# Output projection weights split into other places and earlier, gated products moved, and the first down unit put behind the second up columns

## The chip, the cores and the metric

The kernel runs on one core of one Trainium2 chip. The metric is the device time of one execution in microseconds (us); lower is better. The core has five engines with a queue each: TensorE (PE in the profile), VectorE (DVE), ScalarE (ACT), GpSimd (POOL) and SyncE (SP), which here only starts weight loads. Granted clock means the share of TensorE's full 2.4 GHz that the chip allowed in a stretch.

## What is computed

Two layers over 256 tokens of width 1024 in float32. Each layer is a half-step SwiGLU feed-forward block, an attention block with two kinds of heads (8 stick-breaking, 8 chunked with a relative bias), and a second feed-forward block, with a layer norm after each of the three.

```
x  <- LN1(alpha*x + 1/2 * SwiGLU_1(x))          # width 1024 -> 2816 -> 1024
h  = x @ W_in                                   # q,k,v of both kinds of heads
y  = concat(g_A * headRMS(StickBreak(...)), g_B * headRMS(ChunkAttn(...))) @ W_out
x  <- LN2(alpha*x + y)
x  <- LN3(alpha*x + 1/2 * SwiGLU_2(x))
SwiGLU(x) = (silu(x @ w_gate) * (x @ w_up)) @ w_down
```

## The kernel before

**Split weights.** Every product is made of three matmuls on rounded halves: hi*hi, lo*hi, hi*lo. Weights stream in as *units* of 128 x 2048 float32 (1 MB). SP loads a unit into one of three slots of `raw`; ACT writes its rounded copy into a place of `w_hi` (`split_hi`, L422) and DVE the remainder into the same place of `w_lo` (`split_lo`, L753). There are four places. A raw slot may be loaded again once DVE has made the low part of the unit in it (`lo_ready`); a place may be written again once PE has used the unit there (`unit_used`). PE waits on `lo_ready`. Each engine works its queue in the order in which the code is written: all order around the change is by hand.

**Feed-forward block.** `ffn` takes per step j a gate unit, an up unit and a down unit. Gate and up are products of x (48 matmuls with 256 columns for each unit, `columns`); ACT makes the silu, DVE the gated product (`gated`, signals `hf_done`). The first nine down units are multiplied by Strassen's scheme in seven products of 512 columns, `product(m)`, each accumulated in PSUM bank m; DVE forms sums of weights for it (`weight_sums`: `weight_differences` and `weight_additions`, L768 to L774) and sums of h (`h_sums`), and both are split in hi and lo (`split_pure`, `split_differences`, `split_last_parts`, `high_h`, `low_h`). The last two down units are plain (`pair`). In the second to fourth blocks of the program PE takes the second gate and second up unit before the first down unit. In the program's first block (`count == 0`) PE takes gate 0, up 0, gate 1, products 5, 2, 4, 3 of down 0, then up 1, then products 1, 6, 7.

**Attention block.** Twelve units of W_in, interleaved with the attention of both kinds of heads, then four units of W_out (called W0 to W3 below; `rels` in the code). The softmax of the chunked heads goes in six batches b: PE scores, DVE adds the bias and finds the maximum (`scores`), ACT takes the exponential (`softmax_exp`), DVE normalises, PE transposes (`ca_turn`), and DVE (b 0 to 3) or ACT (b 4, 5) copies back (`turned`). The head outputs are normed (`square`, `head_rstd`, `mix`) and split (`mixed_hi`, `mixed_lo`); each part i of four feeds one W_out unit. PE does W0 for all, W1 for all, then W2 and W3 for token block 0, then W2 and W3 for token block 1.

**Layer norm and the next pair of units.** As soon as a token block's sums are in PSUM (`y_done`), DVE and ACT norm it, PE transposes the result (`turn_x`) and takes the next block's first two units together (`first_pair`, `row_products`). These two must already lie in two places: they are split by `split_hi(..., into=...)` and by `split_second_hi`/`split_second_lo`, the second in two halves. On DVE `split_second_lo` stands ahead of `layer_norm`. Inside the last W_out product of token block 1 stands a transpose of the normed token block 0, so that PE waits there for the norm of token block 0.

SP's loads follow in one queue; `back` says after which unit's low part a slot is free. For the second up unit of the second feed-forward block (raw slot 1) that is the low part of W3.

Of the kernel before, what the change touches and what calls it, by code (L numbers as in the profile page):

```python
# [88 lines left out]
SLOT, FILLED, PER_LAYER = unit_slots()  # L89

# [24 lines left out]
def trunk(nc, x_in, xT_in, stream, ln_gb, mix_g, rel_band, out):  # L115
    ctx = ExitStack()
    with ctx:
# [169 lines left out]
        def phase(l, p):  # L287
            return l * 3 + p
# [128 lines left out]
        def _(act):  # L417
# [26 lines left out]
            def split_second_hi(l, filled, after):  # L444

                act.wait_ge(raw_ready[1], loaded(l, 1, filled))
                act.wait_ge(unit_used, used(l, after))
                for c, done in zip(HALVES, (first_hi, hi_ready)):
                    nc.scalar.activation(w_hi[:, at(0, c)], raw[:, 1, c], ACT.Copy).then_inc(done, 1)

            def split_hi_at(l, rel):
                if rel == ATT0 + WIN_UNITS:
                    act.wait_ge(unit_used, used(l, rel - 2))
                split_hi(l, rel, SLOT[rel], FILLED[rel])

# [35 lines left out]
            def ffn(l, f):  # L491
# [7 lines left out]
                def silu_rows(r, tb, done):  # L499

                    act.wait_ge(*((unit_used, used(l, base + 1)) if tb else (row_done, r + 1)))
                    c = slice(tb * 256, tb * 256 + 256)
                    nc.scalar.activation(sg[:, c], bank[4 + tb][:, 256:512], ACT.Silu).then_inc(done, 1)
# [11 lines left out]
                if r < 0:  # L515
# [3 lines left out]
                    split_hi(l, base + 3, 0, first[0] + 1)  # L519
                    first_unit_hi()  # L520
                    high_h(0)
                    split_differences_hi(l, f, 0)
                else:
# [12 lines left out]
                    split_last_parts_hi(l, f, 0)  # L536
                    split_hi(l, base + 5, 2, first[2] + 1)
# [17 lines left out]
                if r < 0:  # L555
                    step(0)
# [20 lines left out]
                if r < 3 * DEPTH - 2:  # L577
                    split_second_hi(l, first[1] + FP, base + 3 * SF + 3)
# [88 lines left out]
            def attention(l):  # L667
# [47 lines left out]
                split_hi_at(l, ATT0 + 12)  # L715
# [4 lines left out]
                split_hi_at(l, ATT0 + 13)  # L720
# [31 lines left out]
        def _(dve):  # L752
# [49 lines left out]
            def split_half_lo(half, slot=0):  # L802
                c = HALVES[half]
                nc.vector.tensor_tensor(w_lo[:, at(0, c)], raw[:, slot, c], w_hi[:, at(0, c)].bitcast(F32),
                                        ALU.subtract).then_inc((first_lo, lo_ready)[half], 1)

            def split_second_lo(l, p, rel):

                dve.wait_ge(first_hi, phase(l, p) + 1)
                split_half_lo(0, 1)  # L810
                dve.wait_ge(hi_ready, l * UNITS + (rel + 1))
                split_half_lo(1, 1)
# [96 lines left out]
            def ffn(l, f):  # L909
# [25 lines left out]
                def gated_rows(r, tb):  # L935
# [4 lines left out]
                                                   in1=bank[4 + tb][:, 0:256], op0=ALU.mult,  # L940
                                                   op1=ALU.mult).then_inc(row_h_done, 1)

                r = 2 * l + f - 1
                if r < 0:
                    split_lo(l, base + 1, 1)
                    split_lo(l, base + 2, 2)
                    weight_sums(l, f, 0, FILLED[base + 1] + 1)
                    gated(0, 1, bank[7], first=True)
                    h_sums(0)
                    split_pure_lo(l, f, 0)  # L950
                    low_h(0)
                    split_differences_lo(l, f, 0)
                    split_lo(l, base + 3, 0)
# [12 lines left out]
                for j in range(2):  # L966
                    split_last_parts_lo(l, base + 3 * j + 4)
                    if j == 0:
                        split_lo(l, base + 3 * j + 5, 2)
                        weight_sums(l, f, j + 1, FILLED[base + 1] + 2 + j)  # L970
# [3 lines left out]
                    gated(j + 1, 3 * j + 3, bank[7 if r >= 0 and j == 0 else 0])  # L974
# [38 lines left out]
                if not last:  # L1013
                    split_second_lo(l, 2 * f + 1, base + FFN_UNITS + 1)
# [74 lines left out]
            def attention(l):  # L1089
# [22 lines left out]
                normalise(l, 3)  # L1112
                turned(l, 2)
                scores(l, 4)
                normalise(l, 4)
                turned(l, 3)
# [3 lines left out]
                split_lo_at(l, ATT0 + 12)  # L1120
# [3 lines left out]
                split_lo_at(l, ATT0 + 13)  # L1124
                split_lo_at(l, ATT0 + 14)
# [4 lines left out]
                split_lo_into(l, ATT0 + 15, 1, 3)  # L1130
                split_lo_into(l, FFN_BASE[1], 0, 1)
                split_second_lo(l, 2, FFN_BASE[1] + 1)
# [18 lines left out]
        def _(pe):  # L1151
# [64 lines left out]
            def row_products(l, rel, tb, other, count, turn=None):  # L1216

                t = slice(tb * P, (tb + 1) * P)
                w = [tile[:, :].rearrange("p (s c) -> p s c", c=at(other).start - at(0).start)
                     for tile in (w_hi, w_lo)]  # L1220
                s, c0 = divmod(at(0).start, at(other).start - at(0).start)
                o = bank[4 + tb][:, :].rearrange("p (s c) -> p s c", s=2)

                def product(x, part, kc, start=False, stop=False):
                    return plain(o, x[:, kc, t], w[part][:, s:s + 2, c0 + kc * 256:c0 + (kc + 1) * 256], start, stop)
# [19 lines left out]
            def first_pair(l, rel, other, count, units):  # L1245

                turn_x(0, count, 1)
                row_products(l, rel, 0, other, count, lambda half: turn_x(1, count, half))
                last_used(count - 1, units)
                row_products(l, rel, 1, other, count)  # L1250
# [41 lines left out]
            def ffn(l, f, count):  # L1292
# [38 lines left out]
                if count == 0:  # L1331
                    first_columns(l, base, count)
                    columns(l, base + 1, 1, bank[7])
                    step(0, start=True)
                else:
                    first_pair(l, base, 1 if f else 3, count, 2 if f else 1)
# [9 lines left out]
                    columns(l, base + 3, 0, bank[7])  # L1346
                    n = strassen(l, f, 0)
                    pe.wait_ge(hlo_done, it(l, f, 0) + 1)
                    pe.wait_ge(lo_part, 2 * n + 1)
                    product(5, True)  # L1350
                    product(2, True)
                    pe.wait_ge(lo_part, 2 * n + 2)
                    product(4, True)
                    product(3, True, parts_used)
                    pe.wait_ge(lo_ready, split(l, base + 4))
                    product(1, True)
                    product(6, True)
                    pe.wait_ge(hf_done, it(l, f, 1) + 1)
                    product(7, True, unit_used)
# [107 lines left out]
            def attention(l):  # L1467
                first_pair(l, ATT0, 3, phase(l, 1), 1)
# [45 lines left out]
                for i in range(2):  # L1514
                    pe.wait_ge(mlo_done, l * 4 + (i + 1))
                    pe.wait_ge(lo_ready, split(l, rels[i]))
                    for tb in range(2):
                        for half in range(2):
# [3 lines left out]
                            last = down(SLOT[rels[i]], xT_hi, xT_lo, 2 * i, (tb,), start=i == 0, halves=(half,))  # L1522
# [5 lines left out]
                for tb in range(2):  # L1528
                    for i in (2, 3):
# [3 lines left out]
                        for half in range(2):  # L1533
                            turn = (tb, i, half) == (1, 3, 1)
                            last = down(3 if i == 3 else SLOT[rels[i]], xT_hi, xT_lo, 2 * i, (tb,), stop=i == 3,
# [73 lines left out]
```

## Time and profile before

| | us |
|---|---|
| three runs, median | 1018.33 |
| lowest, highest | 1015.13, 1020.71 |
| the profiled execution, time | 1017.5 |
| the profiled execution, span in the trace | 1015.8 |
| PE busy in it | 978.3 |
| DVE busy | 809.2 |
| ACT busy | 566.5 |
| POOL busy | 26.5 |

The span runs from the first to the last instruction of the trace; 1.7 us of the execution's time lie around it. Busy time of an engine is the union of its instructions. A matmul's end in the trace is modelled: back to back, 512-column matmuls start 0.23 us apart and show 0.39 us each, so a row's idle time before a matmul is about 0.16 us less than the delay it stands for. The mean granted clock is 0.989. Layer 0 of the trace is roughly 0 to 498 us: feed-forward 0 to 204, attention to 318, feed-forward to 517; layer 1 follows in the same pattern, its attention ending near 815 us.

### The profile page before, as it was taken

How to read it: one execution, taken by the hardware profiler on the slowest of the kernel's cores; microseconds unless marked ns; L12 is line 12 of the kernel's file. 1: busy time of each engine (PE TensorE's matmuls, PEld its weight loads, DVE VectorE, ACT ScalarE, POOL GpSimd, SP SyncE). 2: the span in 40 equal slices, each digit the busy share in tenths (PEclk: the TensorE clock that was granted, in tenths of full speed). 3: DMA queues.
4: the chain of work that ended last, by engine and by line, in shares of the span. 5: the costliest groups of instructions: out<-in, count | busy, mean ns of one | idle time of the engine just before them, and what ended most of it. 6: DMA issues, size and time to landing. Idle time of an engine off the chain costs nothing.

```text
span 1015.8 us, 17324 instructions
## 1 busy us (share of the span) xinstructions
PE 978.3 (96%) x6744; PEld 905.0 (89%) x6744; DVE 809.2 (80%) x879; ACT 566.5 (56%) x619; POOL 26.5 (3%) x54
## 2 busy tenths in 40 slices
PE   6999999999997999999999999999999979999997
PEld 6899999899985899999888999997999769999996
DVE  4988887754786899887889988876567779988875
ACT  5555554467683555554565555545676646555543
POOL 2000000001100000000000000000010000000000
PEclk9999999999998999999999999999999989999998
DMA  8556644553324556554626574544532346555441
GB/s 328 177 198 239 255 166 168 206 207 125 126 84 165 187 198 221 179 206 166 230 76 234 207 289 166 216 176 168 185 103 106 137 154 220 206 195 206 168 164 42
DMA packets 33788, 184.14 MB, mean 181 GB/s; under 512 B 3792, under 2 KB 3792, under 8 KB 18640
## 3 DMA queue, kind: packets, MB, share of 16 engines
q1 hardware_dynamic: 32112, 173.55, 47.6%
q0 software_dynamic: 1488, 9.45, 2.4%
q8 instruction: 31, 0.51, 0.2%
q10 hardware_dynamic: 144, 0.52, 0.1%
q14 instruction: 13, 0.11, 0.0%
HBM read 182.46 MB, written 1.05 MB: 181 GB/s over the span
## 4 chain that ended last, share of the span: by engine, by line
PE 83%; DVE 9%; DMA 4%; ACT 3%; issue 1%; SPq 0%; DVEq 0%; ACTq 0%
PE bank L1154 24%; PE bank L1155 24%; PE bank L1156 24%; PE bank L1285 8%; DMA raw<-stream 4%; DVE w_lo L755 2%; ACT w_hi L429 1%; PE bank L1212 1%; DVE w_lo L761 1%; DVE xn L845 1%; DVE xn L877 1%; PE bank L1457 1%; ACT scratch L469 0%; DVE stick_t L772 0%; DVE soft_t L919 0%
## 5 line engine op out<-in xcount | busy, mean ns | idle before, releaser
L1154 PE MATMUL bank<-xT_hi,w_hi 128*128 128x256 f32 x1488 | 422.1, 284 | 0.0
L1156 PE MATMUL bank<-xT_hi,w_lo 128*128 128x256 f32 x1488 | 421.0, 283 | 0.0
L1155 PE MATMUL bank<-xT_lo,w_hi 128*128 128x256 f32 x1488 | 421.0, 283 | 0.0
L755 DVE TENSOR_TENSOR w_lo<-raw,w_hi 128x2048 fp32r<-128x2048 f32 x115 | 263.3, 2291 | 72.9 <-ACT w_hi L429 72.6
L429 ACT ACTIVATE w_hi<-raw 128x2048 fp32r<-128x2048 f32 x122 | 232.9, 1911 | 132.3 <-PE bank L1156 129.4
L1155 PEld LDWEIGHTS bank<-xT_lo,w_hi 128*128 128x128 f32 x1488 | 285.2, 192 | 3.1
L1154 PEld LDWEIGHTS bank<-xT_hi,w_hi 128*128 128x128 f32 x1488 | 285.2, 192 | 3.1
L1156 PEld LDWEIGHTS bank<-xT_hi,w_lo 128*128 128x128 f32 x1488 | 285.2, 192 | 0.0
L1154 PE MATMUL bank<-w_hi,h_hi 128*128 128x512 f32 x284 | 112.6, 396 | 4.5 <-DVE h_lo L932 2.4
L1155 PE MATMUL bank<-w_lo,h_hi 128*128 128x512 f32 x284 | 111.9, 394 | 0.0
L1156 PE MATMUL bank<-w_hi,h_lo 128*128 128x512 f32 x284 | 111.0, 391 | 0.0
L497 ACT ACTIVATE scratch<-bank 128x512 f32<-128x512 f32 x41 | 24.5, 598 | 124.4 <-PE bank L1156 123.3
L1154 PE MATMUL bank<-w_hi,xT_hi 128*128 128x256 f32 (+1 forms) x192 | 65.8, 343 | 2.0 <-DVE xT_lo L1086 2.0
L1154 PEld LDWEIGHTS bank<-w_hi,h_hi 128*128 128x128 f32 x284 | 54.0, 190 | 15.2 <-DVE soft_t L919 3.4
L1156 PEld LDWEIGHTS bank<-w_hi,h_lo 128*128 128x128 f32 x284 | 53.6, 189 | 11.9
L799 DVE TENSOR_TENSOR w_lo<-stick_t,w_hi 128x1536 fp32r<-128x1536 f32 x36 | 63.1, 1752 | 0.8 <-ACT w_hi L442 0.8
L1155 PE MATMUL bank<-w_lo,xT_hi 128*128 128x256 f32 (+1 forms) x192 | 61.6, 321 | 0.0
L1156 PE MATMUL bank<-w_hi,xT_lo 128*128 128x256 f32 (+1 forms) x192 | 61.6, 321 | 0.0
L1155 PEld LDWEIGHTS bank<-w_lo,h_hi 128*128 128x128 f32 x284 | 54.1, 190 | 8.3
L919 DVE SCALAR_TENSOR_TENSOR soft_t<-scratch,bank 128x512 f32<-128x512 f32 x41 | 28.2, 687 | 39.7 <-PE bank L1156 39.6
L433 ACT ACTIVATE w_hi<-raw 128x1024 fp32r<-128x1024 f32 x36 | 38.2, 1060 | 27.7 <-PE bank L1156 23.2
L442 ACT ACTIVATE w_hi<-stick_t 128x1536 fp32r<-128x1536 f32 x36 | 53.0, 1472 | 0.0
(151 smaller groups left out, 1219.7 us busy)
## 6 DMA issues: line engine op xcount, KB each, us to landing
raw<-stream SPq DMA_DIRECT2D x110, 1024.0 KB, 4.8
raw<-stream SPq DMA_DIRECT2D x108, 512.0 KB, 4.6
lnp<-ln_gb POOLq DMA_DIRECT2D x6, 1024.0 KB, 5.3
band<-rel_band POOLq DMA_DIRECT2D x2, 1024.0 KB, 9.3
xn<-x POOLq DMA_DIRECT2D x1, 1024.0 KB, 7.4
out<-xn SPq DMA_DIRECT2D x4, 256.0 KB, 2.1
qT<-xT SPq DMA_DIRECT2D x1, 512.0 KB, 4.8
qT<-xT ACTq DMA_DIRECT2D x1, 512.0 KB, 5.0
```

Source lines behind the costliest of these rows:

```text
L429: nc.scalar.activation(w_hi[:, at(slot if into is None else into)], raw[:, slot, :], ACT.Copy).then_inc(hi_ready, 1)
L433: nc.scalar.activation(w_hi[:, at(1, seven(0, 2))], raw[:, 1, 512:1536], ACT.Copy).then_inc(hi_part, 1)
L442: nc.scalar.activation(w_hi[:, at(1, seven(4, 3))], wsum[:, 1024:2560], ACT.Copy).then_inc(hi_ready, 1)
L497: nc.scalar.activation(sg, bank[0][:, :], ACT.Silu).then_inc(silu_done, 1)
L755: nc.vector.tensor_tensor(w_lo[:, at(slot)], raw[:, slot, :], w_hi[:, at(slot)].bitcast(F32), ALU.subtract).then_inc(lo_ready, 1)
L761: nc.vector.tensor_tensor(w_lo[:, at(into)], raw[:, slot, :], w_hi[:, at(into)].bitcast(F32), ALU.subtract).then_inc(lo_ready, 1)
L799: nc.vector.tensor_tensor(w_lo[:, c], wsum[:, 1024:2560], w_hi[:, c].bitcast(F32), ALU.subtract).then_inc(lo_ready, 1)
L919: nc.vector.scalar_tensor_tensor(out=h_pair, in0=sg.rearrange(four, c=2, b=2), scalar=0.5, in1=source[:, :].rearrange(four, c=2, b=2), op0 ...
L1154: nc.tensor.matmul(o, w[0], x[0], start=start, stop=False, skip_group_check=again)
L1155: nc.tensor.matmul(o, w[0], x[1], start=False, stop=False, skip_group_check=again)
L1156: return nc.tensor.matmul(o, w[1], x[0], start=False, stop=stop, skip_group_check=again)
L1285: return nc.tensor.matmul(o, w, x, start=start, stop=stop, skip_group_check=True)
```

## The change

Four things are edited; the number and the kinds of matmuls stay as they are.

1. *W_out.* The raw slots stay, but W0 to W3 go to places 0, 3, 1, 2 (`W_OUT_AT`) where they went to 1, 0, 2, 3. Their splits on ACT stand at other spots: W0 behind `softmax_exp(2)`, W1 behind the squares, W2 behind `softmax_exp(5)`, W3 behind `mixed_hi(0, 0)`. On DVE they stand behind `normalise(3)`, `normalise(4)`, `normalise(5)` and `mixed_lo(0, 1)`. The next block's first pair goes to places 0 and 3 in every block, so `row_products` has one fixed view, and in the second feed-forward block gate and up change sides of the bank.
2. *Program's first block.* Gate 1, up 1 (into bank 6), then all seven products of down 0, with 6 last. The branch is merged with that of the other blocks.
3. *Gated product of step 1.* For j == 0 it stands ahead of `weight_sums` on DVE.
4. *End of the first three feed-forward blocks.* The low split of the next block's first unit is cut in halves with the last gated product between them.

```diff
+W_OUT_AT = (0, 3, 1, 2)
...
+            def w_out_hi(l, i):
+
+                rel = ATT0 + WIN_UNITS + i
+                split_hi(l, rel, SLOT[rel], FILLED[rel], into=W_OUT_AT[i], after=ATT0 + (9, 9, 10, 11)[i])
...
                     split_hi(l, base + 3, 0, first[0] + 1)
+                    high_h(0)
                     first_unit_hi()
-                    high_h(0)
                     split_differences_hi(l, f, 0)
+                    silu(1, 2)
...
                 softmax_exp(l, 2)
+                w_out_hi(l, 0)
                 softmax_exp(l, 3)
                 square(l, 0, 0)
                 square(l, 0, 1)
+                w_out_hi(l, 1)
...
                 softmax_exp(l, 5)
-                split_hi_at(l, ATT0 + 12)
+                w_out_hi(l, 2)
                 turned(l, 4)
                 evacuate(l, 11)
                 turned(l, 5)
                 mixed_hi(l, 0, 0)
-                split_hi_at(l, ATT0 + 13)
+                w_out_hi(l, 3)
                 square(l, 1, 0)
                 mixed_hi(l, 0, 1)
                 square(l, 1, 1)
-                split_hi_at(l, ATT0 + 14)
                 head_rstd(l, 1, 0)
                 head_rstd(l, 1, 1)
-                split_hi(l, ATT0 + 15, 1, FILLED[ATT0 + 15], into=3, after=ATT0 + 1)
-                split_hi(l, FFN_BASE[1], 0, FILLED[FFN_BASE[1]], into=1, after=ATT0 + 12)
                 mixed_hi(l, 1, 0)
+                split_hi(l, FFN_BASE[1], 0, FILLED[FFN_BASE[1]], into=0, after=ATT0 + 12)
                 mixed_hi(l, 1, 1)
-                split_second_hi(l, FILLED[FFN_BASE[1] + 1], ATT0 + 13)
+                split_second_hi(l, FILLED[FFN_BASE[1] + 1], ATT0 + 13, 3)
...
                     if j == 0:
                         split_lo(l, base + 3 * j + 5, 2)
+                        gated(j + 1, 3 * j + 3, bank[6 if r < 0 else 7])
                         weight_sums(l, f, j + 1, FILLED[base + 1] + 2 + j)
...
                 if not last:
-                    split_lo_into(l, base + FFN_UNITS, 0, 3)
+                    dve.wait_ge(hi_ready, l * UNITS + (base + FFN_UNITS + 1))
+                    c = at(3, HALVES[0])
+                    nc.vector.tensor_tensor(w_lo[:, c], raw[:, 0, HALVES[0]], w_hi[:, c].bitcast(F32), ALU.subtract)
                 gated(FP - 1, 3 * SF + 3, bank[4])
+                if not last:
+                    c = at(3, HALVES[1])
+                    nc.vector.tensor_tensor(w_lo[:, c], raw[:, 0, HALVES[1]], w_hi[:, c].bitcast(F32),
+                                            ALU.subtract).then_inc(lo_ready, 1)
...
                 if count == 0:
                     first_columns(l, base, count)
                     columns(l, base + 1, 1, bank[7])
-                    step(0, start=True)
+                    pe.wait_ge(silu_done, it(l, f, 0) + 1)
+                    columns(l, base + 2, 2, bank[0])
+                    u1, order = 6, (5, 2, 4, 3, 1, 7, 6)
```

DVE at the end of layer 0's attention, before. `L1070` to `L1078` are one `mix`, `L1086` is `mixed_lo`, `L761` the low parts of W3 and of the next block's gate unit, `L804` the two halves of `split_second_lo`, `L845` the first operation of the layer norm:

```order
L1070 SCALAR_TENSOR_TENSOR scratch<-bank,scratch 128x512 [waits rsq_done]
L1073 SCALAR_TENSOR_TENSOR ez<-scratch,ez 128x512 [waits newton]
L1078 SCALAR_TENSOR_TENSOR qT<-bank,mixg,ez 128x256 [waits newton]
L1078 SCALAR_TENSOR_TENSOR qT<-bank,mixg,ez 128x256
L1086 TENSOR_TENSOR xT_lo<-qT,xT_hi 128x512 [waits mhi_done] x2
L761 TENSOR_TENSOR w_lo<-raw,w_hi 128x2048 [waits hi_ready] x2
L804 TENSOR_TENSOR w_lo<-raw,w_hi 128x1024 [waits first_hi]
L804 TENSOR_TENSOR w_lo<-raw,w_hi 128x1024 [waits hi_ready]
L845 SCALAR_TENSOR_TENSOR xn,sums<-xn,bank 128x512 [waits y_done,lnp_ready,xn_done]
```

The same place in the changed kernel, from one `mix` earlier (`L764` is a low part into a named place, `L807` and `L851` are what `L804` and `L845` were):

```order
L1099 TENSOR_TENSOR xT_lo<-qT,xT_hi 128x512 [waits mhi_done]
L764 TENSOR_TENSOR w_lo<-raw,w_hi 128x2048 [waits hi_ready]
L1083 SCALAR_TENSOR_TENSOR scratch<-bank,scratch 128x512 [waits rsq_done]
...
L1099 TENSOR_TENSOR xT_lo<-qT,xT_hi 128x512 [waits mhi_done] x2
L764 TENSOR_TENSOR w_lo<-raw,w_hi 128x2048 [waits hi_ready]
L807 TENSOR_TENSOR w_lo<-raw,w_hi 128x1024 [waits first_hi]
L807 TENSOR_TENSOR w_lo<-raw,w_hi 128x1024 [waits hi_ready]
L851 SCALAR_TENSOR_TENSOR xn,sums<-xn,bank 128x512 [waits y_done,lnp_ready,xn_done]
```

W3's low part now stands ahead of the last two `mix`; behind them only the gate unit's and the two halves are left.

DVE at the program's start, before (`L755` splits, `L768` to `L774` weight sums, which wait for the load of down 0, `L919` gated product, `L926` to `L928` sums of h, `L932` low part of h):

```order
L755 TENSOR_TENSOR w_lo<-raw,w_hi 128x2048 [waits hi_ready] x2
L768 TENSOR_TENSOR stick_t<-raw 128x1024 [waits lo_ready,raw_ready1]
L772 TENSOR_TENSOR stick_t<-raw 128x1024
L774 TENSOR_TENSOR stick_t<-raw 128x512
L919 SCALAR_TENSOR_TENSOR soft_t<-scratch,bank 128x2x256 [waits unit_used,silu_done]
L926 TENSOR_TENSOR soft_t<-soft_t 128x256 [waits hf_done]
...
L785 TENSOR_TENSOR w_lo<-raw,w_hi 128x1024 [waits hi_part]
L932 TENSOR_TENSOR h_lo<-soft_t,h_hi 128x896 [waits hhi_done]
```

And in the changed kernel:

```order
L758 TENSOR_TENSOR w_lo<-raw,w_hi 128x2048 [waits hi_ready] x3
L925 SCALAR_TENSOR_TENSOR soft_t<-scratch,bank 128x2x256 [waits unit_used,silu_done]
L932 TENSOR_TENSOR soft_t<-soft_t 128x256 [waits hf_done]
...
L771 TENSOR_TENSOR stick_t<-raw 128x1024 [waits lo_ready,raw_ready1]
L775 TENSOR_TENSOR stick_t<-raw 128x1024
L777 TENSOR_TENSOR stick_t<-raw 128x512
L788 TENSOR_TENSOR w_lo<-raw,w_hi 128x1024 [waits hi_part]
L938 TENSOR_TENSOR h_lo<-soft_t,h_hi 128x896 [waits hhi_done]
```

The third split (up 1), the gated product and the sums of h now stand ahead of the weight sums; on PE, 48 matmuls of up 1 have come between gate 1 and the first product.

## Rows read from the trace of the kernel before

**Rows 1.** All waits of PE: us in total, times, longest.
```profile
PE bank L1212 <- DVE xn L877: 12.8, 5, 6.6
...
PE bank L1154 <- DVE soft_t L919: 2.1, 3, 0.7
PE bank L1154 <- DVE xT_lo L1086: 2.0, 2, 1.4
PE bank L1154 <- DVE hl_lo L1010: 1.5, 3, 0.5
```

**Rows 2.** Busy time in two stretches: PE, PEld, DVE, ACT, POOL, clock, DMA.
```profile
180.00:205.00 25.00, 24.25 (x135) 20.45 (x134) 19.83 (x33) 13.07 (x19) 0.59 (x1) 1.00 0.50 180
...
312.00:335.00 23.00, 17.58 (x77) 14.29 (x76) 15.00 (x32) 9.74 (x16) 0.55 (x1) 0.85 0.55 205
```

**Rows 3.** PE from attention to feed-forward, layer 0: start us, us, engine, line [idle before <-releaser].
```profile
307.44 0.50 PE L1154 MATMUL bank<-w_hi,xT_hi 128*128 128x512 f32 x1 [1.41 <-DVE xT_lo L1086]
...
317.68 0.39 PE L1156 MATMUL bank<-w_hi,xT_lo 128*128 128x512 f32 x1
323.49 1.11 PE L1212 MATMUL bank<-table,xn 128*128 128x128 f32 x4 [5.42 <-DVE xn L877]
...
333.43 0.48 PE L1285 MATMUL bank<-w_hi,xT_hi 128*128 128x512 f32 x1
```

**Rows 4.** DVE over the same stretch.
```profile
295.77 4.49 DVE L755 TENSOR_TENSOR w_lo<-raw,w_hi 128x2048 fp32r<-128x2048 f32 x2
...
307.91 4.49 DVE L761 TENSOR_TENSOR w_lo<-raw,w_hi 128x2048 fp32r<-128x2048 f32 x2
316.36 2.36 DVE L804 TENSOR_TENSOR w_lo<-raw,w_hi 128x1024 fp32r<-128x1024 f32 x2 [3.96 <-ACT w_hi L449]
318.63 0.68 DVE L845 SCALAR_TENSOR_TENSOR xn<-xn,bank 128x512 f32<-128x512 f32 x1
```

**Rows 5.** ACT over the same stretch.
```profile
306.05 1.13 ACT L665 ACTIVATE xT_hi<-qT 128x512 fp32r<-128x512 f32 x2
315.26 2.01 ACT L449 ACTIVATE w_hi<-raw 128x1024 fp32r<-128x1024 f32 x2 [8.08 <-DMA raw<-stream]
```

**Rows 6.** PE from feed-forward to attention, layer 0.
```profile
196.16 0.40 PE L1156 MATMUL bank<-w_hi,hl_lo 128*128 128x512 f32 x1
...
204.70 0.47 PE L1285 MATMUL bank<-w_hi,xT_hi 128*128 128x512 f32 x1
```

**Rows 7.** PE from attention to feed-forward, layer 1.
```profile
815.06 0.39 PE L1156 MATMUL bank<-w_hi,xT_lo 128*128 128x512 f32 x1
...
831.87 0.48 PE L1285 MATMUL bank<-w_hi,xT_hi 128*128 128x512 f32 x1
```

**Rows 8.** DVE and ACT in the softmax batches, layer 0.
```profile
276.93 0.69 DVE L1060 COPY soft_t<-bank 128x512 f32<-128x512 f32 x1 [1.11 <-PE bank L1457]
...
282.81 0.69 DVE L1060 COPY soft_t<-bank 128x512 f32<-128x512 f32 x1 [1.34 <-PE bank L1457]
...
273.23 0.40 ACT L632 ACTIVATE soft_t<-soft_t,nmx 128x128 f32<-128x128 f32 x1 [2.32 <-DVE nmx L1045]
```

**Rows 9.** ACT and PE around the last softmax batch.
```profile
288.12 0.57 ACT L657 ACTIVATE soft_t<-bank 128x512 f32<-128x512 f32 x1
...
289.64 0.60 PE L1457 MATMUL bank<-table,soft_t 128*128 128x128 f32 x4
```

**Rows 10.** PE and ACT at the program's start.
```profile
31.11 0.80 PE L1154 MATMUL bank<-w_hi,h_hi 128*128 128x512 f32 x1 [2.41 <-DVE h_lo L932]
...
34.27 0.40 PE L1155 MATMUL bank<-w_lo,h_hi 128*128 128x512 f32 x1
...
17.96 1.91 ACT L429 ACTIVATE w_hi<-raw 128x2048 fp32r<-128x2048 f32 x1
```

**Rows 11.** DVE in the second feed-forward block.
```profile
352.30 1.22 DVE L768 TENSOR_TENSOR stick_t<-raw 128x1024 f32<-128x1024 f32 x1
```

**Rows 12.** DVE at the end of the first feed-forward block.
```profile
184.40 2.29 DVE L761 TENSOR_TENSOR w_lo<-raw,w_hi 128x2048 fp32r<-128x2048 f32 x1
```

More of the change, by code:

```diff
@@ L442, in split_last_parts_hi, with split_second_hi @@
                 nc.scalar.activation(w_hi[:, at(1, seven(4, 3))], wsum[:, 1024:2560], ACT.Copy).then_inc(hi_ready, 1)
-            def split_second_hi(l, filled, after):
+            def split_second_hi(l, filled, after, into):
                 act.wait_ge(raw_ready[1], loaded(l, 1, filled))
@@ L502, in silu_rows @@
                     c = slice(tb * 256, tb * 256 + 256)
-                    nc.scalar.activation(sg[:, c], bank[4 + tb][:, 256:512], ACT.Silu).then_inc(done, 1)
+                    gate = slice(0, 256) if f else slice(256, 512)
+                    nc.scalar.activation(sg[:, c], bank[4 + tb][:, gate], ACT.Silu).then_inc(done, 1)
                 def high_h(j):
@@ L973, in ffn @@
                         split_lo(l, base + 3 * j + 5, 2)
-                    gated(j + 1, 3 * j + 3, bank[7 if r >= 0 and j == 0 else 0])
+                        gated(j + 1, 3 * j + 3, bank[0])
                     h_sums(j + 1)
@@ L1214, in turn_x, with row_products @@
                 last.then_inc(xt_done, 1)
[L1216 removed]
+            def row_products(l, rel, tb, count, turn=None):
                 t = slice(tb * P, (tb + 1) * P)
[L1219 to L1221 removed]
+                w = [tile[:, :].rearrange("p (s c) -> p s c", s=2)[:, :, UW:] for tile in (w_hi, w_lo)]
                 o = bank[4 + tb][:, :].rearrange("p (s c) -> p s c", s=2)
                 def product(x, part, kc, start=False, stop=False):
[L1225 removed]
+                    return plain(o, x[:, kc, t], w[part][:, :, kc * 256:(kc + 1) * 256], start, stop)
                 pe.wait_ge(lo_ready, split(l, rel + 1))
@@ L1243, in row_products, with first_pair @@
                     last.then_inc(unit_used, 2)
-            def first_pair(l, rel, other, count, units):
+            def first_pair(l, rel, count, units):
                 turn_x(0, count, 1)
-                row_products(l, rel, 0, other, count, lambda half: turn_x(1, count, half))
+                row_products(l, rel, 0, count, lambda half: turn_x(1, count, half))
                 last_used(count - 1, units)
-                row_products(l, rel, 1, other, count)
+                row_products(l, rel, 1, count)
             def first_columns(l, rel, count):
@@ L1345, in ffn @@
                     columns(l, base + 2, 2, bank[0], (1,))
[L1346 to L1359, printed above, removed]
+                    u1, order = 7, (5, 2, 4, 3, 1, 6, 7)
+                columns(l, base + 3, 0, bank[u1])
+                n = strassen(l, f, 0)
+                pe.wait_ge(hlo_done, it(l, f, 0) + 1)
+                for i, m in enumerate(order):
+                    if i == 0:
+                        pe.wait_ge(lo_part, 2 * n + 1)
+                    elif i == 2:
+                        pe.wait_ge(lo_part, 2 * n + 2)
+                    elif i == 4:
+                        pe.wait_ge(lo_ready, split(l, base + 4))
+                    elif i == 6:
+                        pe.wait_ge(hf_done, it(l, f, 1) + 1)
+                    product(m, True, {3: parts_used, order[6]: unit_used}.get(m))
                 with pe.Fori(1, SF - 1) as j:
@@ L1521, in attention @@
                                 pe.wait_ge(mix_done, l * 4 + 2)
-                            last = down(SLOT[rels[i]], xT_hi, xT_lo, 2 * i, (tb,), start=i == 0, halves=(half,))
+                            last = down(W_OUT_AT[i], xT_hi, xT_lo, 2 * i, (tb,), start=i == 0, halves=(half,))
                         if tb == 1:
@@ L1534, in attention @@
                             turn = (tb, i, half) == (1, 3, 1)
-                            last = down(3 if i == 3 else SLOT[rels[i]], xT_hi, xT_lo, 2 * i, (tb,), stop=i == 3,
+                            last = down(W_OUT_AT[i], xT_hi, xT_lo, 2 * i, (tb,), stop=i == 3,
                                         halves=(half,), turn=phase(l, 2) if turn else None)
```

50 lines of the change are left out of this document (24 added, 26 removed).

## Prediction

> **What bounds the kernel now.** I read the page first: PE is busy for 978 of 1015.8 us, so time can only come from the 37.5 us in which it idles, or from matmuls that run slowly. The list of all waits of PE tells where [rows 1]: 12.8 us for `xn`, the normed block that it transposes, 2.1 for the gated product (three times), 2.0 for the low part of the mixed heads (twice), 1.5 for the low part of the last h (three times). Then I looked at two stretches side by side [rows 2]: from 180 to 205, around a layer norm, PE works 24.25 of 25 us at full clock; from 312 to 335, around the norm after attention, 17.58 of 23, and the granted clock is 0.85. One kind of norm is covered, the other is not. PE's own rows in order of time give each delay.
>
> **The norm after attention.** In layer 0 PE stops behind the matmul at 317.68 and goes on at 323.49 with the transposes of the normed block [rows 3]. DVE is why [rows 4]: its first operation of the norm (L845) starts at 318.63 only, right behind the two halves of the second up unit's low part, which start at 316.36 after 3.96 us of idling for ACT, and ACT waited 8.08 us for that unit's load [rows 5]. The load waits for the low part of W3, the first of the two splits that start at 307.91. So the chain is: W3's low part, load, high part, low part, norm, PE.
>
> The change puts W3's low part ahead of the last two `mix`, where so far two splits start at 295.77 [rows 4]; it is done near 298. The second up unit's load is then issued near 298 in place of 310; from 310.1 (end of W3's low part, 307.91 + 2.2) to ACT's start at 315.26 it took 5.2, so it is there by 303.5. What holds the split next is place 3, free when PE ends W1. PE's first matmul of W2 is at 307.44 [rows 3], after a wait; without it W1 ends near 305.9, with 0.4 of lateness (below) 306.3. The two halves cost ACT 2.01 [rows 5] and DVE's second half ends 1.2 after that: DVE is free for the norm at 309.6. The first sum that it needs is there 18 matmuls after W2 starts: (317.68 - 307.44)/44 = 0.233 each, so at 306.3 + 4.2 = 310.5, the second at 311.9. From the second L845, 0.6 behind the first at 318.63, to the transposes at 323.49 is 4.25 [rows 3, 4]: the normed half is there at 316.2. PE has 21 matmuls to do from the second sum on, 4.9 us: it arrives at 316.8. No wait, with 0.6 to spare, and 0.9 to spare on DVE.
>
> What that is worth: I compare the same piece of PE's program at the covered norm, from the last matmul before the transposes to the first row product of token block 1: 196.16 to 204.70, 8.54 us [rows 6]. After attention it takes 317.68 to 333.43, 15.75, in layer 0 and 815.06 to 831.87, 16.81, in layer 1 [rows 3, 7]. The gains are 7.2 and 8.3. They are more than the idle time, because the clock falls to the lower of its two levels behind the gap (four transposes take 1.1 us at 323.49 and 0.6 at 289.64) [rows 3, 9].
>
> The Trainium skill (TensorE: Matmul & The Clock Gate, part 1 on the HAM clock gate) says that the number of slow matmuls after a cold start varies from run to run of one kernel, 6, 11 or 14 in its example. No run here shows it yet. By it the share of the clock in these two gains would be 1.2 to 2.8 us each (an estimate from that page with 0.2 us for a slow matmul) rather than what this one execution shows, and the sum could move by about 2 us.
>
> **The wait at W2.** 1.41 us in layer 0, 0.6 in layer 1 [rows 1, 3]. A record's modelled end laps 0.16 over the next start, so the delays are 1.6 and 0.8. `mixed_hi` for part 1 starts at 306.05 on ACT [rows 5]; ahead of it stand the high parts of W3 and of the gate unit. Now it stands ahead of both, so it comes at least one split (1.8) earlier. I take the whole 2.4.
>
> **What the earlier splits cost.** Two low parts of 2.2 us more, those of W0 and W1, now stand between DVE's softmax steps; W2's stands where W0's stood. `turned` of batch 2 starts at 276.93 after 1.11 idle, that of batch 3 at 282.81 after 1.34 [rows 8]. W0's split makes the first 1.1 late; the exponential behind it is then some 0.8 late; W1's makes the second 0.8 + 2.2 - 1.34 = 1.7 late, and batch 5's exponential on ACT some 1.3. ACT's `turned` of batch 4, from 288.12 to 288.69, then ends near 289.95, and PE's last softmax transposes, at 289.64, need it [rows 9]: 0.4 us late with the signal. Bounds: nothing, if the idle takes it all, or 4.4 per layer, both on the path. I take 0.4, which the two rows give. On ACT the two high parts (1.8 each) go into idle such as the 2.32 ahead of batch 3's exponential [rows 8].
>
> The Trainium skill (the same page, on engine queue depths) says that ScalarE and VectorE work their queues strictly in order. By that rule alone each inserted split makes everything behind it late by its whole length, which is the upper bound of 4.4; the idle rows above speak for less.
>
> **Program's start.** PE idles 2.41 before the first product of down 0, for h's low part, which came behind the weight sums, which wait for the load; then seven matmuls take 3.16 (31.11 to 34.27) where seven take 1.63 at full clock [rows 10]. The delay is 2.41 + 0.16 + 1.5 = 4.1. Now 48 matmuls of up 1 lie between, and in this kernel's other blocks the same order runs. Up 1's weights must be there: ACT made their high part from 17.96 on [rows 10], so DVE can make the low part near 20. The products start near 34.5, and the last thing they needed was ready at 31.1, one split of 2.2 later now. I take all 4.1. Bounds: 2.6 (if the clock still falls for another reason) to 4.1.
>
> **Gated product of step 1.** In three blocks DVE starts the weight sums at 352.30 (and its like) [rows 11], the gated product follows them, and PE waits 0.7 for it [rows 1]. Put first it is done near 353. The gain is the wait, 2.1 + 3 x 0.16 = 2.6. The weight sums come 0.7 later; their first user on PE is a whole gate unit away.
>
> **End of three blocks.** The low part from 184.40 on takes 2.2 [rows 12], the gated product starts behind it, and PE waits 0.5 for what follows [rows 1]. With a half ahead it can start 1.1 earlier; the other half stands behind it, still ahead of the low part of h. The delay is 1.5 + 3 x 0.16 = 2.0; I take 1.8. Bounds: 1.0 to 2.0, since the second half (1.2) may push the low part of h.
>
> **Sum.** 7.2 + 8.3 + 2.4 - 0.8 + 4.1 + 2.6 + 1.8 = 25.6. Against its own execution, 1017.5 - 25.6 = 991.9. That execution is 0.8 below the median of the runs; from the median 1018.33 - 25.6 = 992.7.
>
> **Rivals.**
>
> *The norm stays partly uncovered* (0.14). The two halves of the second up unit still stand ahead of the norm on DVE, and now wait for place 3, that is for PE itself. If ACT or DVE comes to them 2 us late, PE loses about 1.4 per layer: 995.5. If 4 late, the gap is as long as that at the start, which dropped the clock, and costs 3.4 + 1.6 per layer: 1002.7. For it: DVE has 0.9 to spare only. Against: the late parts hang on PE's own end of W1, so they move with it.
>
> *The softmax chain becomes the bound* (0.11). Both added splits on the path, 4.4 in place of 0.4 per layer: 1000.7. For it: DVE's steps and ACT's wait for each other, so lateness is handed on. Against it the idle of [rows 8].
>
> *The change does not do what it says* (0.03). If the load and not the order held the norm, for instance because loads of several units share the queue and the second up unit still lands past 310, only the start, gated product and block ends are left: 1018.3 - 8.5 = 1009.8.
>
> *Slower* (0.03). The high part of W0 now stands ahead of `softmax_exp` of batch 3 on ACT's queue and waits there for W0's load; if that comes late, the exponential, PE's transposes and all behind are late by as much, less the 2.32 - 1.8 of idle there [rows 8]. To end 0.5% above 1018.3, 30.7 us must be lost again, so the load would have to be some 16 us late in each layer; it decides from there, and below it only lessens the gain. Against: a load took 5.2 above.
>
> Within 0.5% of before (0.03) is what most of that lateness would give. The forecast has 0.66.
>
> **How the numbers follow.** 0.5% of 1018.3 is 5.1 us, about what a measurement of this kernel can tell from no change. The forecast 992.7; with no lateness and the whole waits it would be 991.7, and the runs before went down to 3.2 below their median: 988. The upper end, 1003, takes in the partly uncovered norm and the softmax chain, and leaves out 0.09. Faster: the first four cases, 0.94; same 0.03; slower 0.03.
>
> **What would show it.** In the changed trace: PE's wait for `xn` falls from 12.8 to under 2; no fall of the clock near 310 to 325 and near 30; the distance from the last matmul before the transposes to the first row product of token block 1 is near 8.5 at all norms; the waits for the gated product, for the low part of the last h and at W2 are gone; a new one of some 0.4 stands at the last softmax transposes. I am wrong if DVE's first operation of the norm still starts behind an idle stretch for ACT, or if PE waits for `soft_t` in the last softmax batches by more than 1 us.

## The result, and the profile after

The changed kernel took 990.69 us (median of 4 runs, 990.01 to 991.45), the kernel before, on the same chip, 1018.09 (4 runs, 1015.13 to 1020.71): a ratio of 0.9732, with a 95% interval from 0.9704 to 0.976. That is 27.4 us less by the medians, and 26.1 by the two spans (1015.8 and 989.7); the prediction was 25.6. The page of the changed kernel, its line of busy times and that of the granted clock:

```profile
PE 971.1 (98%) x6744; PEld 901.7 (91%) x6744; DVE 808.6 (82%) x882; ACT 566.4 (57%) x619; POOL 26.6 (3%) x54
...
PEclk9999999999999999999999999999999999999998
```

The number of matmuls is the same; PE is busy 7.2 us less than before (978.3): three stretches of slow matmuls are gone, some 1.5 us each, one at the start and one behind each norm after attention. The other 2.7 were not traced; every wait that is gone also takes 0.16 of modelled busy time with it. All waits of PE in the changed kernel, the answer to [rows 1]:

```profile
PE bank L1296 <- ACT w_hi L742: 9.5, 1, 9.5
PE bank L1225 <- DVE xn L883: 1.1, 5, 0.3
PE bank L1470 <- ACT soft_t L661: 0.6, 2, 0.3
```

The first is the program's first load, which the change does not touch. The wait for `xn` has gone from 12.8 to 1.1; those for the gated product, the mixed heads and the last h are no longer there, nor is that for `h_lo` at the start. The last line is new. The stretches of [rows 2] in the changed kernel, with the program's start ahead (the end of the attention is near 312 now):

```profile
12.00:32.00 20.00, 20.00 (x158) 20.00 (x158) 15.97 (x15) 11.79 (x10) 0.87 (x1) 1.00 0.69 256
180.00:205.00 25.00, 24.74 (x125) 20.37 (x124) 20.93 (x36) 12.44 (x19) 0.59 (x1) 1.00 0.52 170
312.00:335.00 23.00, 22.81 (x145) 20.20 (x144) 20.32 (x30) 14.54 (x19) 0.55 (x1) 1.00 0.29 97
```

The clock is 1.00 in all three, and the norm after attention is as full as the one in front of it. PE in order of time, as in [rows 3] and [rows 7]; the first row is the start of W2 in layer 0, `L1225` the transposes of the normed block and `L1296` the row products:

```profile
302.15 0.39 PE L1167 MATMUL bank<-w_hi,xT_hi 128*128 128x512 f32 x1
...
312.12 0.39 PE L1169 MATMUL bank<-w_hi,xT_lo 128*128 128x512 f32 x1
312.36 0.60 PE L1225 MATMUL bank<-table,xn 128*128 128x128 f32 x4
...
320.58 0.48 PE L1296 MATMUL bank<-w_hi,xT_hi 128*128 128x512 f32 x1
...
798.36 0.39 PE L1169 MATMUL bank<-w_hi,xT_lo 128*128 128x512 f32 x1
...
806.82 0.48 PE L1296 MATMUL bank<-w_hi,xT_hi 128*128 128x512 f32 x1
```

From the last matmul before the transposes to the first row product of token block 1 it is 8.46 us in both layers (312.12 to 320.58, 798.36 to 806.82), against 8.54 at the covered norm of before and 15.75 and 16.81 at these two. No idle stands before W2's first matmul or before the transposes.

### The profile page after: what moved, and what is told of

It reads as the page before. It is cut to its first block, busy times and chain, and to the rows that moved or that the text cites. A ratio compares the mean times of both kernels' runs of the same rounds, so it can differ in the third digit from the quotient of the medians.

```text
span 989.7 us, 17324 instructions
## 1 busy us (share of the span) xinstructions
PE 971.1 (98%) x6744; PEld 901.7 (91%) x6744; DVE 808.6 (82%) x882; ACT 566.4 (57%) x619; POOL 26.6 (3%) x54
## 4 chain that ended last, share of the span: by engine, by line
PE 87%; DVE 8%; ACT 3%; issue 1%; DMA 1%; POOL 0%; DVEq 0%; SPq 0%; POOLq 0%
PE bank L1167 27%; PE bank L1168 27%; PE bank L1169 27%; PE bank L1296 6%; ACT soft_t L636 1%; DVE w_lo L758 1%; DVE w_lo L764 1%; PE bank L1225 1%; ACT w_hi L430 1%; DVE qT L864 1%; DVE mx L1056 1%; DMA raw<-stream 1%; DVE soft_t L1053 1%; DVE xn L883 1%; DVE xT_lo L825 1%
## 5 line engine op out<-in xcount | busy, mean ns | idle before, releaser
L758 DVE TENSOR_TENSOR w_lo<-raw,w_hi 128x2048 fp32r<-128x2048 f32 x109 | 249.7, 2291 | 74.7 <-ACT w_hi L430 74.3
```

What stands on the lines that cost most here:

```text
L758: nc.vector.tensor_tensor(w_lo[:, at(slot)], raw[:, slot, :], w_hi[:, at(slot)].bitcast(F32), ALU.subtract).then_inc(lo_ready, 1)
```

## Why DVE is in time now

DVE of the changed kernel, as in [rows 4]: W3's low part, the first operation of the last mixes, the two halves, the two first operations of the norm.

```profile
292.05 2.28 DVE L764 TENSOR_TENSOR w_lo<-raw,w_hi 128x2048 fp32r<-128x2048 f32 x1
295.35 0.69 DVE L1083 SCALAR_TENSOR_TENSOR scratch<-bank,scratch 128x512 f32<-128x512 f32 x1 [1.01 <-ACT scratch L657]
...
303.57 2.35 DVE L807 TENSOR_TENSOR w_lo<-raw,w_hi 128x1024 fp32r<-128x1024 f32 x2
306.54 0.69 DVE L851 SCALAR_TENSOR_TENSOR xn<-xn,bank 128x512 f32<-128x512 f32 x1 [0.61 <-PE bank L1169]
...
307.79 0.69 DVE L851 SCALAR_TENSOR_TENSOR xn<-xn,bank 128x512 f32<-128x512 f32 x1 [0.56 <-PE bank L1169]
```

SP's loads of the changed kernel, and ACT's two halves, as in [rows 5]:

```profile
294.50 0.86 SPq L313 DMA_DIRECT2D raw<-stream  x2
```

```profile
302.41 2.01 ACT L450 ACTIVATE w_hi<-raw 128x1024 fp32r<-128x1024 f32 x2 [1.68 <-PE bank L1169]
```

The second up unit's load is issued at 294.50, right behind W3's low part (292.05 + 2.2). ACT no longer waits 8.08 for it, but 1.68 for PE to leave place 3. DVE is then idle for 0.61 before the norm: it waits for PE now, and PE not for it.

## Experiments

**Are the parts worth what the sum says?** Four kernels, each the kernel before with one of the four edits (on one chip; there the kernel before took 1018.13, median of 24 runs from 1014.93 to 1021.57). The diffs here and below are cut to the lines that matter.

*Start alone.* Beside the order on PE shown here, it moves the high part of h, the second silu, the low split of up 1, the first gated products and the weight sums of this block to where the changed kernel has them.

```diff
-                    step(0, start=True)
+                    pe.wait_ge(silu_done, it(l, f, 0) + 1)
+                    columns(l, base + 2, 2, bank[0])
+                    u1, order = 6, (5, 2, 4, 3, 1, 7, 6)
```

> The kernel before with the new order at the program's start alone. Theory A (each part returns its own wait, and the parts add up): 4.1 us less than before, of which 2.6 are the idle time in front of the first product of down 0 and 1.5 the slow matmuls behind it; PE has no wait and no fall of the clock near 30 us. Theory B (the parts hang together, PE only reaches the next wait sooner): less than 2 us.

Measured: 1013.96 (9 runs), ratio 0.9959 [0.9945, 0.9974], 4.2 us less. The first product starts at 35.03 without a wait.

*Gated product of step 1 first.*

```diff
                     if j == 0:
                         split_lo(l, base + 3 * j + 5, 2)
+                        if r >= 0:
+                            gated(j + 1, 3 * j + 3, bank[7])
                         weight_sums(l, f, j + 1, FILLED[base + 1] + 2 + j)
```

> The kernel before with the gated product of step 1 ahead of the weight sums in the second to fourth blocks alone. Theory A: 2.6 us less, PE's waits for soft_t (2.1 us, three times) are gone. Theory B: the weight sums, now 0.7 later, hold PE at the products of step 1, and nothing is gained.

Measured: 1014.82 (10 runs), ratio 0.9969 [0.9953, 0.9984], 3.3 us less. The waits for `soft_t` are gone.

*Low split of the next first unit in halves.*

```diff
-                    split_lo_into(l, base + FFN_UNITS, 0, 3)
...
+                    nc.vector.tensor_tensor(w_lo[:, c], raw[:, 0, HALVES[0]], w_hi[:, c].bitcast(F32), ALU.subtract)
                 gated(FP - 1, 3 * SF + 3, bank[4])
...
+                    nc.vector.tensor_tensor(w_lo[:, c], raw[:, 0, HALVES[1]], w_hi[:, c].bitcast(F32),
+                                            ALU.subtract).then_inc(lo_ready, 1)
```

> The kernel before with the low part at the end of three blocks cut in halves alone. Theory A: 1.8 to 2.0 us less, PE's waits for hl_lo (1.5 us, three times) are gone. Theory B: the second half pushes the low part of h, and 1.0 or less is gained.

Measured: 1014.99 (12 runs), ratio 0.9969 [0.9954, 0.9983], 3.1 us less. The waits for `hl_lo` are gone.

*W_out alone*: all hunks of the change with `w_out_hi`, `w_out_lo`, `W_OUT_AT` and `into`; start, gated product and block ends as before.

> The kernel before with the W_out part alone (places, earlier splits, first pair in places 0 and 3). Theory A: 17.1 us less (7.2 + 8.3 + 2.4 - 0.8), span near 998.7; the gap of 2.4 us at the program's start stays, with about seven slow matmuls behind it, and the waits for soft_t and hl_lo stay. Theory B (parts hang together): less than 14 us here, and the four runs of this job do not add up to the 27.4 us of the whole.

Measured: 1000.66 (5 runs), ratio 0.9828 [0.9807, 0.9849], 17.5 us less. All waits of PE in it, without the first load:

```profile
PE bank L1161 <- DVE h_lo L939: 3.6, 1, 3.6
PE bank L1161 <- DVE soft_t L926: 2.1, 3, 0.7
PE bank L1161 <- DVE hl_lo L1017: 1.5, 3, 0.5
PE bank L1219 <- DVE xn L884: 1.1, 5, 0.3
PE bank L1462 <- ACT soft_t L662: 0.5, 2, 0.3
```

This edit takes away the two long waits for `xn` and those for `xT_lo`, and brings the new one for ACT's `soft_t`; the other three stand. The four gains add up to 4.2 + 3.3 + 3.1 + 17.5 = 28.1, against 27.4 for the whole, which was measured on another chip: nothing is lost or won by their being together that these runs could tell.

**Is it the order of W3's low part that uncovers the norm?** The changed kernel with that one line back behind the last mixes (another set of runs, before 1016.29, 9 runs; the next three kernels belong to it). The changed kernel itself was not in this set. It took 990.69 and 990.52 on two other chips, and the one kernel that ran both in this set and on one of those chips took 989.46 and 989.80 (W2 later, below). So differences from 990.69 may be some 0.5 us too small or too large.

```diff
                 mixed_lo(l, 0, 1)
-                w_out_lo(l, 3)
                 mix(l, 1, 0)
                 mix(l, 1, 1)
                 mixed_lo(l, 1, 0)
                 mixed_lo(l, 1, 1)
+                w_out_lo(l, 3)
```

> The changed kernel with one row moved back: DVE makes W3's low part behind the last two mixes and the last two low parts of the heads. Theory A (the chain W3's low part, load of the second up unit, its split, the norm on DVE): the load is issued near 303.7 instead of 294, DVE starts the norm near 312 instead of 306.5, PE waits about 4.5 us for the normed block in each layer and the clock falls again: 6 us per layer, 12 in all, near 1003 us. Theory B (the order of the splits on ACT, or the places, made the gain): less than 3 us.

Measured: 1002.82 (4 runs), ratio 0.9863 [0.9845, 0.9882]; 12.1 us over the changed kernel's 990.69 (13.3 by the two ratios). SP, ACT and PE of this kernel in layer 0, three views:

```profile
303.18 0.86 SPq L313 DMA_DIRECT2D raw<-stream  x2
```

```profile
308.05 2.01 ACT L450 ACTIVATE w_hi<-raw 128x1024 fp32r<-128x1024 f32 x2 [7.96 <-DMA raw<-stream]
```

```profile
311.49 0.39 PE L1169 MATMUL bank<-w_hi,xT_lo 128*128 128x512 f32 x1
316.28 1.12 PE L1225 MATMUL bank<-table,xn 128*128 128x128 f32 x4 [4.40 <-DVE xn L883]
...
326.31 0.47 PE L1296 MATMUL bank<-w_hi,xT_hi 128*128 128x512 f32 x1
```

And its stretches, whose seventh figure is the clock:

```profile
312.00:316.00 4.00, 0.00 (x0) 0.00 (x0) 3.43 (x11) 1.74 (x4) 0.00 (x0) 0.75 0.95 352
316.00:320.00 4.00, 3.72 (x13) 3.23 (x14) 2.70 (x8) 1.03 (x2) 0.00 (x0) 0.50 0.01 2
320.00:324.00 4.00, 4.00 (x17) 3.23 (x17) 3.89 (x9) 3.07 (x6) 0.00 (x0) 0.90 0.00 0
```

The whole chain of [rows 3], [rows 4] and [rows 5] is back: the load is issued 8.7 us later (303.18, not 294.50; this execution runs 0.6 ahead of the changed kernel's), ACT waits 7.96 for it and PE 4.40 for the norm. The piece from the last matmul to the first row product of token block 1 takes 14.82 (311.49 to 326.31) where it took 8.46: 6.4 more, of which 4.40 + 0.16 are the gap and 1.8 are left for the matmuls at the lower clock (0.50 of full speed from 316 to 320). PE rests from 311.9 on; the clock is down for half of the slice 312:316 already and comes back in 320:324. So in the changed kernel this one line's place is worth some 12 us. What it would bring alone in the kernel before was not run.

**What hides the earlier splits?** Two kernels double one of the early low parts (the same subtraction into the same place, once more), and one puts W2's split later.

```diff
                 normalise(l, 3)
...
+                nc.vector.tensor_tensor(w_lo[:, at(0)], raw[:, SLOT[rel], :], w_hi[:, at(0)].bitcast(F32),
+                                        ALU.subtract).then_inc(extra, 1)
+                dve.wait_ge(extra, l + 1)
                 w_out_lo(l, 0)
```

> The changed kernel with W0's low part made twice on DVE, 2.2 us more ahead of turned of batch 2. It computes the same. Theory A (the two splits have used up the idle time of the softmax steps, so the wait at the last softmax transposes grows by what is added): PE's wait there grows from 0.3 to about 2.5 us per layer, 4.4 us more in all. Theory B (idle time is left): less than 1.5 us more.

Measured: 995.23 (4 runs), ratio 0.979 [0.9773, 0.9808]; 4.5 us over the changed kernel. Its waits of PE that are new or longer:

```profile
PE bank L1476 <- ACT soft_t L662: 2.9, 2, 1.4
PE bank L1476 <- DVE soft_t L1074: 1.9, 2, 1.0
```

DVE's copy back of batch 2 (`turned`) starts 4.5 behind the first W0 split here (270.84 to 275.37) and 2.2 behind it in the changed kernel (271.59 to 273.79), and nothing takes that up: PE waits 1.0 and up to 1.4 in each layer at the softmax transposes of two batches, and the kernel loses 4.5 / 2 = 2.25 per layer for a split of 2.3. The idle of [rows 8] was used up by the change itself. DVE still idles between the two places, in the changed kernel and, second row, in this one:

```profile
277.16 0.17 DVE L1066 RECIPROCAL rinv<-se 128x2 f32<-128x2 f32 x1 [1.16 <-ACT soft_t L636]
278.74 0.17 DVE L1067 RECIPROCAL rinv<-se 128x2 f32<-128x2 f32 x1 [1.16 <-ACT soft_t L637]
```

This idle is for ACT's exponential, which itself waits for DVE's maximum; it is 1.16 in the kernel before too (at 280.57), so it took up nothing. The idle of 1.11 and 1.34 in [rows 8], which was for PE, is gone in the changed kernel: that is what took up part of the first two splits.

```diff
                 mixed_lo(l, 0, 1)
...
+                nc.vector.tensor_tensor(w_lo[:, at(2)], raw[:, SLOT[rel], :], w_hi[:, at(2)].bitcast(F32),
+                                        ALU.subtract).then_inc(extra, 1)
+                dve.wait_ge(extra, l + 1)
                 w_out_lo(l, 3)
```

> The changed kernel with W3's low part made twice on DVE, 2.2 us more ahead of the last two mixes, where DVE now idles 1.0 us. It computes the same. Theory A (margin left: 0.6 us of idle in front of the norm and 0.2 behind it): DVE comes 1.2 us later to the norm, PE loses 0.2 to 0.6 us per layer, no fall of the clock, 0.4 to 1.2 us in all. Theory B (the last two mixes or the low parts of the heads are on PE's path): 2.4 us or more in all.

Measured: 990.77 (4 runs), ratio 0.9748 [0.9731, 0.9765]; 0.1 over the changed kernel, where 0.4 to 1.2 were expected. Its waits of PE are those of the changed kernel (1.1 for `xn`, 0.6 for ACT's `soft_t`), so no loss is seen; one of some 0.6 could not be told between the sets. DVE in it, from the second W3 split to the norm:

```profile
293.40 2.29 DVE L765 TENSOR_TENSOR w_lo<-raw,w_hi 128x2048 fp32r<-128x2048 f32 x1
295.61 0.68 DVE L1084 SCALAR_TENSOR_TENSOR scratch<-bank,scratch 128x512 f32<-128x512 f32 x1
...
306.10 0.68 DVE L852 SCALAR_TENSOR_TENSOR xn<-xn,bank 128x512 f32<-128x512 f32 x1
...
306.82 0.69 DVE L852 SCALAR_TENSOR_TENSOR xn<-xn,bank 128x512 f32<-128x512 f32 x1
```

This execution runs 0.97 us ahead of the changed kernel's (its first W3 split starts at 291.08, the other's at 292.05). With that added, the last mixes are 1.23 late (295.61 against 295.35), the first operation of the norm 0.53 (306.10 against 306.54), the second 0.0 (306.82 against 307.79). The 2.3 us are used up by the three idle stretches of the changed kernel's DVE, shown above: 1.01 ahead of the mixes, 0.61 ahead of the norm and 0.56 between its first two operations. The third is the one that the expectation had left out: it allowed 0.2 behind the start of the norm.

```diff
                 softmax_exp(l, 5)
-                w_out_hi(l, 2)
                 turned(l, 4)
+                w_out_hi(l, 2)
                 evacuate(l, 11)
...
                 normalise(l, 5)
-                w_out_lo(l, 2)
-                mixed_lo(l, 0, 0)
                 mix(l, 0, 1)
+                mixed_lo(l, 0, 0)
+                w_out_lo(l, 2)
                 mixed_lo(l, 0, 1)
```

> The changed kernel with W2's high part behind turned of batch 4 on ACT, and W2's low part behind the second mix on DVE, where PE does not need it yet. Theory A (the 0.3 us waits at the last softmax transposes and a hiccup of 0.1 at the second half of W0 are all that is lost there): 0.8 us less in all, no wait of PE for soft_t of ACT. Theory B (PE waits at the next place, for mix or the low part of the heads): no change or up to 0.5 us more.

Measured: 989.46 (5 runs), ratio 0.9734 [0.9719, 0.9748]; its wait for `soft_t` is gone. Since 1.2 us between two sets of runs is little, it was run again beside the changed kernel itself.

> The changed kernel, unchanged, beside the next one on the same chip. Theory A (the gain is what it was: 0.9732 of before) expects 990.7 and an interval inside 0.970 to 0.976. Rival: if it comes out near 989.5, the 1.2 us that the kernel with W2 later was under it in the other run was the chip and not the order.

> W2's high part behind ACT's turned of batch 4, its low part behind the second mix and mixed_lo(0, 0) on DVE, the rest as changed. Theory A (the 0.4 us per layer that PE waits at the last softmax transposes is the cost of W2's high part ahead of turned on ACT) expects 0.6 to 0.8 us under the changed kernel of the same chip. Rival (the wait was off the path, or comes back later) expects no difference within 0.3.

Measured there (before 1018.04, 9 runs): the changed kernel 990.52 (5 runs, 990.35 to 990.91), ratio 0.973 [0.9717, 0.9744]; with W2 later 989.8 (5 runs, 989.22 to 990.41), ratio 0.9721 [0.9708, 0.9734]. PE at the last softmax transposes, in the changed kernel and then in this one:

```profile
285.01 0.63 PE L1470 MATMUL bank<-table,soft_t 128*128 128x128 f32 x4 [0.28 <-ACT soft_t L661]
```

```profile
284.96 0.64 PE L1470 MATMUL bank<-table,soft_t 128*128 128x128 f32 x4
```

ACT of the kernel with W2 later, where the copy of batch 4 now stands ahead of the split:

```profile
282.89 0.58 ACT L661 ACTIVATE soft_t<-bank 128x512 f32<-128x512 f32 x1
283.37 1.91 ACT L430 ACTIVATE w_hi<-raw 128x2048 fp32r<-128x2048 f32 x1
```

The wait is gone and 0.7 us with it, about what its two records of 0.28 + 0.16 each (0.9) ask for. The two ranges of runs overlap by 0.06 (the one starts at 990.35, the other ends at 990.41), so the gain is small, but the medians on one chip show it. W2's high part stood ahead of this copy in the kernel before too; there the copy was early enough to bear it.

## Why the prediction was right

- **Norm after attention, 7.2 + 8.3.** Right in mechanism and size: 7.3 and 8.35 by the same two marks, and DVE idles 0.61 ahead of the norm where 0.9 to spare was worked out. The rival "partly uncovered" did not come: the late parts hang on PE's own end of W1, as argued. The case of 4 us late can be held against the experiment on W3's low part. There DVE's second operation of the norm is 4.9 late (312.03, with 0.6 added, against 307.79) and PE's gap is 4.40 + 0.16, so PE had 0.3 to spare, not 0.6; the kernel lost 6.05 per layer. The rival's 3.4 + 1.6 has the same shape.
- **W2, 2.4.** Both waits are gone in the changed kernel and in W_out alone. That kernel as a whole gave 17.5 for the 17.1 of 7.2 + 8.3 + 2.4 - 0.8; the 2.4 was not measured by itself.
- **Earlier splits, -0.8.** The wait came where it was put, at the last softmax transposes, with 0.28 + 0.16 = 0.44 per layer. Its steps came too. Counted from PE's transposes of batch 2 (276.23 before, 272.09 in the changed kernel), DVE's copy of batch 2 is 1.0 late, the exponential behind it 0.7, the copy of batch 3 1.5, and batch 5's exponential 1.2, where 1.1, 0.8, 1.7 and 1.3 were worked out. The doubled W0 split shows how close the upper bound of 4.4 was: the next 2.3 us of DVE work there cost 2.25.
- **Start, 4.1.** 4.2 measured alone [2.6 to 5.6 by its interval]. The term was built on a gap of 2.41, the shortest of four seen with this start (next section); the same working with the others, 3.35 to 4.27, gives 5.1 to 6.0. That the two figures are so close is in part luck.
- **Gated product, 2.6, and block ends, 1.8.** Alone they gave 3.3 [1.6 to 4.8] and 3.1 [1.7 to 4.7]. The waits that they were to remove are gone in the traces; that the medians give 0.7 and 1.3 more is within what the kernel before moves from run to run, and not settled.
- **Sum.** 25.6 against 26.1 by spans. The 1.3 us more by medians are the choice of executions: the profiled one of the kernel before was 0.6 below its median (1017.5 and 1018.09), that of the changed kernel 0.8 above (991.45 and 990.69).

## What the runs showed of the hardware

*A load's arrival moves the first product.* DVE of the kernel before at the weight sums, and below it the same row of the kernel with the gated product first, whose start is the same code:

```profile
24.37 1.23 DVE L768 TENSOR_TENSOR stick_t<-raw 128x1024 f32<-128x1024 f32 x1 [5.94 <-DMA raw<-stream]
```

```profile
25.38 1.23 DVE L768 TENSOR_TENSOR stick_t<-raw 128x1024 f32<-128x1024 f32 x1 [7.07 <-DMA raw<-stream]
```

The load of down 0 was there 1.0 us later, and PE's first product began at 32.12 where it had begun at 31.11. In four executions with this start (before, gated product first, halves, W_out alone) the weight sums began at 24.37, 25.38, 24.96 and 25.18, the first product 6.7 behind each, and PE idled 2.41, 4.27, 3.35 and 3.65. What makes the spread of the runs is not settled by this. Those of before spread over 6.6 us (24 runs), those with the new start alone over 3.0 (9 runs), those of the changed kernel over 0.6 to 1.4; but those of W_out alone, which has the old start, over 2.0 only (5 runs). The long runs of before also show less clock: 1019.75 us and more at a mean of 0.987 or 0.988, 1018.18 and less at 0.991 or 0.992.

*The clock's fall is not tied to the moment at which PE resumes.* PE of the kernel with the gated product first, and of the one with halves, at the same products:

```profile
32.12 0.50 PE L1157 MATMUL bank<-w_hi,h_hi 128*128 128x512 f32 x1 [4.27 <-DVE h_lo L932]
32.46 0.57 PE L1158 MATMUL bank<-w_lo,h_hi 128*128 128x512 f32 x1
32.83 0.63 PE L1159 MATMUL bank<-w_hi,h_lo 128*128 128x512 f32 x1
```

```profile
31.70 0.50 PE L1160 MATMUL bank<-w_hi,h_hi 128*128 128x512 f32 x1 [3.35 <-DVE h_lo L932]
32.05 0.40 PE L1161 MATMUL bank<-w_lo,h_hi 128*128 128x512 f32 x1
...
32.99 0.42 PE L1162 MATMUL bank<-w_hi,h_lo 128*128 128x512 f32 x1
33.21 0.62 PE L1160 MATMUL bank<-w_hi,h_hi 128*128 128x512 f32 x1
```

At 2.4 GHz such matmuls start 0.23 apart, at 1.2 GHz 0.43. Behind a gap of 4.27 the second one is the first slow one; behind 3.35 six go by at full speed and the seventh is slow; behind the 2.41 of [rows 10] the first one is. In the kernel with the new start alone, a wait of 2.11 at W2 was enough:

```profile
304.72 0.50 PE L1156 MATMUL bank<-w_hi,xT_hi 128*128 128x512 f32 x1 [2.11 <-DVE xT_lo L1088]
...
305.52 0.62 PE L1156 MATMUL bank<-w_hi,xT_hi 128*128 128x512 f32 x1
...
308.50 0.59 PE L1157 MATMUL bank<-w_lo,xT_hi 128*128 128x512 f32 x1
308.93 0.39 PE L1158 MATMUL bank<-w_hi,xT_lo 128*128 128x512 f32 x1
```

The eight from 305.52 to 308.50 are slow, 1.6 us on top of the wait; behind the waits of 1.41, 1.69 and 1.35 at the same place, in the kernel before and in those with the gated product first and with halves, no matmul is slow. In the experiment on W3's low part the clock fell while PE rested (0.75 in the slice 312:316, where PE did nothing). The Trainium skill (TensorE: Matmul & The Clock Gate, part 1) says that the number of slow matmuls varies from run to run. The traces agree that it isn't fixed, though the counts seen here lie closer together than the page's 6 to 14: seven in [rows 10], eight at W2, nine behind the gap of 4.27 (two of them in part), and behind that of 3.35 six with four of 256 columns after them. The time lost is 1.4 to 1.6 us each time; what moves more is where the slow ones begin.

## What to carry to other kernels

When several buffers are refilled through one queue, look which instruction frees the slot of the transfer that ends last, and move that one: here the place of a single 2.3 us subtraction was worth 12 us in a kernel that gained 27, since it set when the load was issued on which the norm's engine later waited. A gap of TensorE costs more than its length once the clock falls behind it: 1.4 to 1.8 us more behind the gaps of 2.1 to 6.6 us that were worked out here, nothing behind those of 1.7 and less. Slack is a property of a place: a 2.3 us instruction cost all of its length between two softmax steps and nothing that could be told 20 us further on. The engine's idle rows tell the two apart only if one looks at what they wait for: idle for an engine that in turn waits for this one, as the 1.16 us for ACT, takes up nothing.
